# A hybrid decoder layer on one core: raw weights requested by GpSimd, twelve slots in the last passes, differences spread anew, another order in the first tile

## The chip, the cores and the metric

The kernel runs on one core of a Trainium2 chip. TensorE multiplies, ScalarE and VectorE prepare operands and work up results, GpSimd (POOL in the profile) helps them, SyncE (SP) requests most transfers. The metric is the device time of one execution in microseconds; lower is better.

## The reference

One inference step of a decoder layer for a prompt of 2048 tokens with 16 meta tokens, and for 8 samples of 8 tokens. The weights are the same for all; everything is fp32.

```python
h = rmsnorm(x, g_pre)
p = h @ w_in + b_in          # q_a k_a v_a z_a | q_m k_m v_m o_m z_m i_m f_m | g_a g_b
y_a = window_attention(q_a, k_a, v_a) * silu(z_a)     # 128 window, 16 meta keys, sinks
y_m = sigmoid(o_m) * mlstm(q_m, k_m, v_m, i_m, f_m) * silu(z_m)    # 4 heads of 256
merged = sigmoid(g_a) * (y_a @ w_pa) + sigmoid(g_b) * (y_m @ w_pb)
x = x + rmsnorm(merged @ w_out, g_post)
```

Returned are the new x of both groups, the window and meta keys and values, and the mLSTM states.

## The kernel before

**Stage 1** (to about 853 us) walks over the 17 tiles of 128 tokens: norm, projection of the attention's columns, attention. For the first tile ScalarE takes the mean square (`square`, L863) and the root (L865), VectorE scales a diagonal matrix with 1/root (`diagonal`, L1067), TensorE transposes the tile with it (`scale_row`, L1354), VectorE multiplies by g_pre (L1074), ScalarE rounds the result to fp32r (`split_made`, L873: the upper half), GpSimd takes input minus upper (`pool_split_h`, L298: the lower half), and TensorE multiplies upper by upper, upper by lower and lower by upper (L308 to L310; `block_b` 264 columns, `block_a` 384). The weights of the tile come in chunks, which ScalarE (L228) and VectorE split in the same way.

**Stage 2** (`stream`) is ten passes, each over all tokens with one weight matrix of 1024 by 1024: ZM, H0 to H3, GA, PA, GB, PB, OUT. Each computes a product by seven multiplications of quarter matrices in place of eight, 60 products a pass. A product is twelve matmuls of 128x512 on L2782, L2784 and L2785, in four quarters. During H0 to H3 the mLSTM of one head runs beside the products (for instance ScalarE's copy of the scores, L2365).

A pass needs seven weight blocks in the order T3, B22, B11, B21, T2, T1, T4, each in four units; unit x of a pass is x = 0 to 27. The B blocks are quarters of the weights, the T blocks are differences or sums of quarters. From H1 on the T blocks come from differences made in the kernel, in 64 chunks: ScalarE requests the four quarters of a chunk (`load_dif`), GpSimd subtracts four times (L2202 to L2208), ScalarE stores (`store_dif`). The list `DIF_AT` says beside which product.

A unit goes through these steps, each put at a product by a rule:

1. SyncE asks for the raw 256 KB into one of `NW` = 6 slots `waiting` (`load_unit`, L2023), after the slot's last user is lowered: `if v - NW >= RING: wait_unit(sp, v - NW)`.
2. ScalarE rounds it into the weight slot (L2297), once TensorE has left that slot: two units a product, from 6 products before the boundary (`unit_split_at`).
3. GpSimd (L2195) or VectorE (L2460) subtracts. In GB and OUT GpSimd has every second unit, in the other passes from H0 on every fourth (x = 3, 7, 11, ...); the rule is `lower_by_dve`.
4. TensorE waits for it before the quarter that uses it: T2 at product 5 of the pass, T1 (x = 20 to 23) at product 6, T4 at product 10.

Each engine's instructions stand in one fixed order, written by loops over the product number q. What waits in it holds up all behind it. SyncE's order has in addition the operands of the products (`next_operand`), three products ahead.

## Time and profile before

| | |
|---|---|
| median of 3 runs | 2869.46 us (2867.12 to 2875.72) |
| time of the profiled execution | 2862.34 us |
| its span, first to last instruction | 2860.3 us |
| mean granted TensorE clock | 0.987 |
| first product of ZM, H0, H1, H2, H3 | 857.2, 1016.2, 1257.0, 1495.7, 1733.7 us |
| first product of GA, PA, GB, PB, OUT | 1970.9, 2142.8, 2314.2, 2482.7, 2668.4 us |

The time of an execution is the span and what lies around it. Times of the trace are counted from the first instruction.

### The profile page before, as it was taken

What the parts mean: (1) busy time and instruction counts of PE and PEld (TensorE: products, weight loads), DVE (VectorE), ACT (ScalarE), POOL (GpSimd) and SP (SyncE); (2) the same over time, 40 slices, a digit from 0 to 9 for tenths busy, and PEclk for the clock granted to TensorE, in tenths of its full rate; (3) what the DMA queues carried; (4) which work ended last, traced back from release to release, by engine and by line L of the source; (5) the groups of instructions that cost most, each with busy time, mean ns of one, the idle gap of its engine ahead of it and who ended that gap; (6) DMA issues with size and microseconds to landing.
All of it is one profiled execution on the core that took longest, in us unless ns stands there. A gap on an engine that the chain in (4) does not pass through costs nothing.

```text
span 2860.3 us, 46433 instructions
## 1 busy us (share of the span) xinstructions
PE 2739.6 (96%) x15620; PEld 2285.6 (80%) x15620; DVE 1652.5 (58%) x4103; ACT 937.9 (33%) x2291; POOL 766.4 (27%) x1064
## 2 busy tenths in 40 slices
PE   6999999999999989999999999999999999999898
PEld 5888888888888767877886887888877878778686
DVE  5776665555653254465465556556247653577787
ACT  5774444444440021131122213114123231333443
POOL 3333533534540021132222223122000020122422
PEclk9999999999999999999999999999999999999999
DMA  8665565545777888898898889789786577956634
GB/s 302 237 223 165 174 207 190 184 166 191 235 225 260 284 303 264 268 333 256 279 291 299 263 286 319 252 263 321 252 293 212 184 276 242 325 194 220 221 142 152
DMA packets 410525, 697.46 MB, mean 244 GB/s; under 512 B 31778, under 2 KB 177575, under 8 KB 410260
## 3 DMA queue, kind: packets, MB, share of 16 engines
q1 hardware_dynamic: 298724, 526.72, 56.0%
q10 hardware_dynamic: 108848, 158.46, 16.2%
q0 software_dynamic: 2720, 9.32, 1.0%
q8 instruction: 128, 2.10, 0.3%
q14 instruction: 105, 0.86, 0.1%
HBM read 526.87 MB, written 169.48 MB: 243 GB/s over the span
## 4 chain that ended last, share of the span: by engine, by line
PE 56%; DMA 8%; DVE 2%; SPq 2%; issue 1%; ACT 1%; POOL 1%; ACTq 0%; POOLq 0%; DVEq 0%
PE bank_second L2782 7%; PE bank_second L2785 7%; PE bank_second L2784 7%; PE bank_third L2782 5%; PE bank_first L2782 5%; PE bank_third L2785 5%; PE bank_first L2785 5%; PE bank_third L2784 5%; PE bank_first L2784 5%; DMA st_waiting<-l_blocks_in 3%; DMA st_waiting<-difs_t 2%; PE st_bank_n L2830 2%; PE st_bank_u L2834 2%; DMA a_all<-sh_t 1%; DMA a_all<-hh_t 1%
## 5 line engine op out<-in xcount | busy, mean ns | idle before, releaser
L2782 PE MATMUL bank_second<-w_all,a_all 128*128 128x512 f32 x736 | 299.1, 406 | 7.0 <-DMA a_all<-sh_t 4.5
L2785 PE MATMUL bank_second<-w_all,a_all 128*128 128x512 f32 x736 | 289.2, 393 | 0.0
L2784 PE MATMUL bank_second<-w_all,a_all 128*128 128x512 f32 x736 | 288.6, 392 | 0.0
L2195 POOL TENSOR_TENSOR w_all<-st_waiting,w_all 128x512 fp32r<-128x512 f32 x57 | 79.3, 1393 | 607.6 <-ACT w_all L2297 607.6
L2365 ACT ACTIVATE mx_qkt<-st_bank_t 128x512 f32<-128x512 f32 x68 | 40.7, 599 | 570.8 <-PE st_bank_t L2805 565.4
L2782 PE MATMUL bank_third<-w_all,a_all 128*128 128x512 f32 x464 | 191.1, 412 | 25.1 <-POOL w_all L2195 10.5
L2782 PE MATMUL bank_first<-w_all,a_all 128*128 128x512 f32 x496 | 199.0, 401 | 8.7 <-DMA a_all<-hh_t 4.3
L2297 ACT ACTIVATE w_all<-st_waiting 128x512 fp32r<-128x512 f32 x184 | 110.4, 626 | 257.7 <-PE bank_first L2785 143.5
L2785 PE MATMUL bank_first<-w_all,a_all 128*128 128x512 f32 x496 | 193.7, 391 | 0.0
L2784 PE MATMUL bank_first<-w_all,a_all 128*128 128x512 f32 x496 | 193.2, 390 | 0.0
L2202 POOL TENSOR_TENSOR h_raw<-h_raw 128x256 f32<-128x256 f32 x64 | 50.2, 785 | 533.5 <-DMA h_raw<-l_blocks_in 533.5
L308 PE MATMUL bank_first<-w_all,a_all 128*128 128x384 f32 x544 | 189.3, 348 | 0.0
L2785 PE MATMUL bank_third<-w_all,a_all 128*128 128x512 f32 x464 | 183.6, 396 | 0.0
L2784 PE MATMUL bank_third<-w_all,a_all 128*128 128x512 f32 x464 | 183.1, 395 | 0.0
L309 PE MATMUL bank_first<-w_all,a_all 128*128 128x384 f32 x544 | 182.0, 335 | 0.0
L310 PE MATMUL bank_first<-w_all,a_all 128*128 128x384 f32 x544 | 182.0, 335 | 0.0
L924 ACT ACTIVATE at_sm<-at_sm,at_nmx 128x208 f32<-128x208 f32 x272 | 124.1, 457 | 153.8 <-DVE at_nmx L1145 153.7
L2782 PEld LDWEIGHTS bank_second<-w_all,a_all 128*128 128x128 f32 x736 | 139.6, 190 | 41.2 <-issue 6.4
L2785 PEld LDWEIGHTS bank_second<-w_all,a_all 128*128 128x128 f32 x736 | 139.3, 189 | 30.2
L2784 PEld LDWEIGHTS bank_second<-w_all,a_all 128*128 128x128 f32 x736 | 139.6, 190 | 27.1
L2516 DVE TENSOR_TENSOR st_u<-bank_second,st_t 128x512 f32<-128x512 f32 x80 | 55.1, 689 | 161.4 <-PE bank_second L2785 161.4
L317 PE MATMUL bank_third<-w_all,a_all 128*128 128x256 f32 (+1 forms) x480 | 147.7, 308 | 0.2 <-POOL a_all L298 0.2
(386 smaller groups left out, 7262.9 us busy)
## 6 DMA issues: line engine op xcount, KB each, us to landing
a_all<-sh_t SPq DMA_DIRECT2D x224, 512.0 KB, 5.2
a_all<-hh_t SPq DMA_DIRECT2D x180, 512.0 KB, 5.5
a_all<-hh_t ACTq DMA_DIRECT2D x104, 512.0 KB, 4.9
st_waiting<-difs_t SPq DMA_DIRECT2D x148, 256.0 KB, 6.9
h_raw<-l_blocks_in ACTq DMA_DIRECT2D x64, 512.0 KB, 5.6
difs_t<-h_raw ACTq DMA_DIRECT2D x64, 512.0 KB, 6.3
st_waiting<-l_blocks_in SPq DMA_DIRECT2D x108, 256.0 KB, 6.5
hh_t<-a_all SPq DMA_DIRECT2D x34, 512.0 KB, 6.1
```

What stands on the lines that cost most here:

```text
L308: nc.tensor.matmul(out, hi[:, j], k.w_hi[:, j, col:col + n], start=(j == 0), stop=False)
L309: nc.tensor.matmul(out, hi[:, j], k.w_lo[:, j, col:col + n], start=False, stop=False)
L310: last = nc.tensor.matmul(out, lo[:, j], k.w_hi[:, j, col:col + n], start=False, stop=(j == KT - 1))
L317: nc.tensor.matmul(out, hi[:, j], k.w_hi[:, j, col:col + n], start=(j == 0), stop=False)
L924: nc.scalar.activation(sm[:, g, :], sm[:, g, :], ACT.Exp, bias=nmx[:, g:g + 1], scale=HD ** -0.5, accum_out=rs[:, g:g + 1]).then_inc(exp_r ...
L2195: G.tensor_tensor(unit_half(v, 1), unit_view(v), unit_half(v, 0).bitcast(F32), ALU.subtract).then_inc(k.lower_done, 1)
L2297: A.activation(unit_half(v, 0), unit_view(v), ACT.Copy).then_inc(k.upper_done, 1)
L2782: T.matmul(bank_view(bank, at), hi, weight_row(k, at, 0, t), start=fresh and t == 0, stop=False, skip_group_check=True)
L2784: T.matmul(bank_view(bank, at), hi, weight_row(k, at, 1, t), start=False, stop=False, skip_group_check=True)
L2785: last = T.matmul(bank_view(bank, at), lo, weight_row(k, at, 0, t), start=False, stop=t == KH - 1, skip_group_check=True)
L2830: T.matmul(p_n[:, 0:MD + 1], qat[:, j, :], cn[:, h % 2, j, :], start=(j == 0), stop=False)
L2834: q = T.matmul(p_u[j][:, 0:MD + 1], kw[:, j * P:(j + 1) * P], vaug(n), start=True, stop=True)
```

## The change

It has four parts.

- **Requests.** `load_unit` moves from SyncE to GpSimd, where it stands ahead of the lower halves of the same product.
- **Tail.** From PA on there are twelve raw slots (six more in memory which the mLSTM has left), the rounding takes three units a product, the lower half stands one product after the rounding, and the requests of the first twelve units start at product 40 of the pass before.
- **Differences.** 14 chunks stand in H0 at products 6, 9, ..., then 16, 15, 15 in H1 to H3 from product 8 on, one in 2.8 products, and 4 in GA. Load and store stand 2 products to either side of the subtractions, not 3.
- **First tile.** ScalarE takes one root of a constant first. Its splitting of chunk 4 comes before `square(1)`, and VectorE's of chunks 2 and 3 before `diagonal(1)`. TensorE runs a block as eight matmuls upper by upper, eight upper by lower, eight lower by upper, the last in step with GpSimd's pairs.

The diff, cut to these parts:

```diff
@@ -751,7 +752,10 @@
             pool.wait_ge(ones_set, 1)
-            pool_split_h(nc, k, 0, 0, None)
+            pool.wait_ge(k.h_hi_ready, 1)
+            for j in range(0, KT, 2):
+                q = nc.gpsimd.tensor_tensor(k.h_lo[:, 0, j:j + 2], k.h_raw[:, 0, j:j + 2], k.h_hi[:, 0, j:j + 2].bitcast(F32), ALU.subtract)
+                q.then_inc(first_lo if j + 2 < KT else k.h_lo_ready, 1)
             pool_split_h(nc, k, 1, 1, None)
@@ -877,16 +881,16 @@
             act.wait_ge(eps_set, 1)
+            nc.scalar.activation(sd[:, 1:2], eps[:, 0:1], ACT.Sqrt)
             square(0)
...
             split_made(0, None)
-            for c in range(2, 4):
+            for c in range(2, 5):
                 act_split_chunk(nc, k, c)
             square(1)
-            act_split_chunk(nc, k, 4)
             split_made(1, None)
@@ -1082,10 +1086,10 @@
                             ALU.subtract).then_inc(gate_lo, 1)
-            dve_split_chunk(nc, k, 1)
+            for c in range(1, 4):
+                dve_split_chunk(nc, k, c)
             diagonal(1)
-            for c in range(2, 5):
-                dve_split_chunk(nc, k, c)
+            dve_split_chunk(nc, k, 4)
             normed(1)
@@ -1398,10 +1402,29 @@
             pe.wait_ge(ones_set, 1)
+            def first_block(out, col, n, chunks, between):
+                hi, lo = k.h_hi[:, 0], k.h_lo[:, 0]
+                pe.wait_ge(k.w_hi_ready, chunks)
+                pe.wait_ge(k.h_hi_ready, 1)
+                for j in range(KT):
+                    T.matmul(out, hi[:, j], k.w_hi[:, j, col:col + n], start=(j == 0), stop=False)
+                between()
+                pe.wait_ge(k.w_lo_ready, chunks)
+                for j in range(KT):
+                    T.matmul(out, hi[:, j], k.w_lo[:, j, col:col + n], start=False, stop=False)
+                for j in range(KT):
+                    if j % 2 == 0 and j + 2 < KT:
+                        pe.wait_ge(first_lo, j // 2 + 1)
+                    elif j % 2 == 0:
+                        pe.wait_ge(k.h_lo_ready, 1)
+                    last = T.matmul(out, lo[:, j], k.w_hi[:, j, col:col + n], start=False, stop=(j == KT - 1))
+                return last
             scale_row(0)
-            block_b(0, 0, 0, True)
-            scale_row(1)
-            block_a(0, 0, 0, True)
+            pe.wait_ge(gate_hi, 1)
+            first_block(p_b[:, 0:W + GATES], attn_base(0) + ZC, W + GATES, k.AT[0] + 2, lambda: pe.wait_ge(gate_lo, 1)).then_inc(proj_b, 1)
+            first_block(p_a[:, 0:ZC], attn_base(0), ZC, k.AT[0] + 5, lambda: scale_row(1)).then_inc(proj_a, 1)
             scale_row(2)
@@ -1595,7 +1618,13 @@
 LOADED_AHEAD = 3
-DIF_AT = {c: N_PROD * H0 + 4 + ((c - DIF_FIRST) * 9 // 2 if c < DIF_FIRST + 8 else 37 + (c - DIF_FIRST - 8) * 18 // 5) for c in range(DIF_FIRST, N_DIF)}
+TAIL = N_UNIT * PA
+DIF_LEAD = 2
+DIF_PLACES = [N_PROD * H0 + 6 + 3 * i for i in range(14)]
+for _s, _n in ((H1, 16), (H2, 15), (H3, 15)):
+    DIF_PLACES += [N_PROD * _s + 8 + i * 14 // 5 for i in range(_n)]
+DIF_PLACES += [N_PROD * GA + 14 + 8 * i for i in range(4)]
+DIF_AT = {c: DIF_PLACES[c - DIF_FIRST] for c in range(DIF_FIRST, N_DIF)}
 DIF_NOW = {q: c for c, q in DIF_AT.items()}
@@ -1752,7 +1781,31 @@
         return -3 if x < EARLY + KH else 5 + (x - EARLY - KH) // 2
-    return N_PROD * s - 6 + x // 2
+    return N_PROD * s - 6 + (x // 3 if s >= PA else x // 2)
+def unit_lowered_at(v):
+    return unit_split_at(v) + (1 if v >= TAIL else 0)
+def waiting_slot(v):
+    return (v - TAIL) % (2 * NW) if v >= TAIL else (v - RING) % NW
+def former_unit(v):
+    before = v - 2 * NW if v - 2 * NW >= TAIL else v - NW
+    if v >= TAIL and v - 2 * NW < TAIL:
+        before = v - NW if v < TAIL + NW else None
+    return before if before is not None and before >= RING else None
+def unit_landed(v):
+    turns = 0
+    while v is not None:
+        turns, v = turns + 1, former_unit(v)
+    return 16 * turns
@@ -1766,12 +1819,16 @@
         return -4 if x < RING + NW else unit_split_at(v) - 1
+    if s >= PA:
+        return N_PROD * (s - 1) + 40 + x if x < 2 * NW else unit_split_at(v) - 2
     return N_PROD * (s - 1) + 46 + x if x < NW else unit_split_at(v) - 1
-SPLITS_AT, LOADS_AT = {}, {}
+SPLITS_AT, LOWERS_AT, LOADS_AT = {}, {}, {}
 for _v in range(EARLY, N_UNITS):
     SPLITS_AT.setdefault(unit_split_at(_v), []).append(_v)
+    LOWERS_AT.setdefault(unit_lowered_at(_v), []).append(_v)
     if _v >= RING:
@@ -2012,15 +2071,6 @@
                     load_operand(sp, k, q)
-            def load_unit(v):
-                s, block, kt = v // N_UNIT, NEEDED[v % N_UNIT // KH], v % KH
-                if 2 * KH * s >= DIF_FIRST and block not in RAW_OF:
-                    for out in dif_out:
-                        sp.wait_ge(out, 16 * (KH * s + kt - DIF_FIRST // 2 + 1))
-                if v - NW >= RING:
-                    wait_unit(sp, v - NW)
-                sp.dma_start(waiting[:, (v - RING) % NW], unit_source(k, v)).then_inc(unit_in[(v - RING) % NW], 16)
@@ -2195,6 +2243,21 @@
+            def load_unit(v):
+                s, block, kt = v // N_UNIT, NEEDED[v % N_UNIT // KH], v % KH
+                if 2 * KH * s >= DIF_FIRST and block not in RAW_OF:
+                    for out in dif_out:
+                        pool.wait_ge(out, 16 * (KH * s + kt - DIF_FIRST // 2 + 1))
+                if former_unit(v) is not None:
+                    wait_unit(pool, former_unit(v))
+                at = waiting_slot(v)
+                if v == TAIL + NW:
+                    pool.wait_ge(state_out, 16 * (MH + 2))
+                    pool.wait_ge(cs_out, 16 * NB * MH)
+                    for i in range(2):
+                        pool.wait_ge(y_out[i], 16 * N_TILES // 2)
+                pool.dma_start(waiting[:, at] if at < NW else more_waiting[:, at - NW], unit_source(k, v)).then_inc(unit_in[at], 16)
             def differences(c):
@@ -2242,10 +2307,12 @@
                         finish(g, row)
+                for v in LOADS_AT.get(q, ()):
+                    load_unit(v)
                 if q == N_PROD * PB:
...
                         load_pa(N_ITEM * PB + row, 0 if row == 0 else 1)
-                for v in SPLITS_AT.get(q, ()):
+                for v in LOWERS_AT.get(q, ()):
                     if not lower_by_dve(v):
@@ -2411,10 +2478,10 @@
                         A.activation(t1[:, :], bank_x[:, :], ACT.Copy).then_inc(t1_ready, 1)
-                if q + 3 in DIF_NOW:
-                    load_dif(DIF_NOW[q + 3])
-                if q - 3 in DIF_NOW:
-                    store_dif(DIF_NOW[q - 3])
+                if q + DIF_LEAD in DIF_NOW:
+                    load_dif(DIF_NOW[q + DIF_LEAD])
+                if q - DIF_LEAD in DIF_NOW:
+                    store_dif(DIF_NOW[q - DIF_LEAD])
                 mixer_first(q)
```

How this moves instructions, at three places.

GpSimd at the change from H0 to H1, before (`w_all` and `w_early` are the weight slots, `h_raw` the two buffers of the differences, L2195 a lower half):

```order
L2195 TENSOR_TENSOR w_all<-st_waiting,w_all 128x512
L2202 TENSOR_TENSOR h_raw<-h_raw 128x256
L2204 TENSOR_TENSOR h_raw<-h_raw 128x256
L2206 TENSOR_TENSOR h_raw<-h_raw 128x256
L2208 TENSOR_TENSOR h_raw<-h_raw 128x256
L2195 TENSOR_TENSOR w_all<-st_waiting,w_all 128x512
L2195 TENSOR_TENSOR w_early<-st_waiting,w_early 128x512
L2202 TENSOR_TENSOR h_raw<-h_raw 128x256
L2204 TENSOR_TENSOR h_raw<-h_raw 128x256
L2206 TENSOR_TENSOR h_raw<-h_raw 128x256
L2208 TENSOR_TENSOR h_raw<-h_raw 128x256
```

and now (L2243 is the lower half, L2259 a request; the first row is x = 3):

```order
L2243 TENSOR_TENSOR w_all<-st_waiting,w_all 128x512
L2259 DMA st_waiting<-l_blocks_in 128x512 x4
L2243 TENSOR_TENSOR w_all<-st_waiting,w_all 128x512
L2259 DMA st_waiting<-l_blocks_in 128x512 x4
L2243 TENSOR_TENSOR w_early<-st_waiting,w_early 128x512
L2259 DMA st_waiting<-l_blocks_in 128x512 x2
L2259 DMA st_waiting<-difs_t 128x512 x2
L2243 TENSOR_TENSOR w_all<-st_waiting,w_all 128x512
L2259 DMA st_waiting<-difs_t 128x512 x4
L2243 TENSOR_TENSOR w_early<-st_waiting,w_early 128x512
L2259 DMA st_waiting<-difs_t 128x512 x4
L2243 TENSOR_TENSOR w_all<-st_waiting,w_all 128x512
```

The subtractions have left the boundary, and between two lower halves stand the four requests of the next group.

GpSimd in OUT, before, around its first final addition (L2233):

```order
L2195 TENSOR_TENSOR w_early<-st_waiting,w_early 128x512 x2
L2195 TENSOR_TENSOR w_all<-st_waiting,w_all 128x512 x3
L2227 TENSOR_TENSOR st_c<-st_c,st_e 128x1024
L2195 TENSOR_TENSOR w_all<-st_waiting,w_all 128x512 x2
L2227 TENSOR_TENSOR st_c<-st_c,st_e 128x1024
L2195 TENSOR_TENSOR w_all<-st_waiting,w_all 128x512 x2
L2233 TENSOR_TENSOR st_e<-st_c,st_e 128x1024
L2195 TENSOR_TENSOR w_all<-st_waiting,w_all 128x512
L2195 TENSOR_TENSOR w_all<-st_waiting,w_all 128x2x256 x2
```

and now (L2243 a lower half, L2290 the addition that belongs to PB, L2296 the final addition):

```order
L2259 DMA st_more_waiting<-difs_t 128x512 x3
L2243 TENSOR_TENSOR w_all<-st_more_waiting,w_all 128x512
L2259 DMA st_more_waiting<-difs_t 128x512 x3
L2243 TENSOR_TENSOR w_all<-st_waiting,w_all 128x512 x2
L2259 DMA st_waiting<-difs_t 128x512 x3
L2243 TENSOR_TENSOR w_all<-st_waiting,w_all 128x512
L2290 TENSOR_TENSOR st_c<-st_c,st_e 128x1024
L2259 DMA st_waiting<-difs_t 128x512
L2243 TENSOR_TENSOR w_all<-st_more_waiting,w_all 128x512 x3
L2290 TENSOR_TENSOR st_c<-st_c,st_e 128x1024
L2243 TENSOR_TENSOR w_all<-st_waiting,w_all 128x2x256 x2
L2296 TENSOR_TENSOR st_e<-st_c,st_e 128x1024 x17
```

All lower halves of the pass stand ahead of the first final addition; before, three stood behind it.

ScalarE at the start, before:

```order
L863 ACT_TABLE_LOAD
L863 ACTIVATE w_plain,at_ss<-w_plain 128x4x256
L865 ACT_TABLE_LOAD
L865 ACTIVATE at_sd<-at_ss,at_eps 128x1
L882 ACTIVATE w_all<-scan_wif 128x8x8
L228 ACTIVATE w_all<-stage 128x8x128 x2
L873 ACTIVATE a_all<-h_raw 128x1024
L228 ACTIVATE w_all<-stage 128x8x128 x2
L863 ACTIVATE w_plain,at_ss<-w_plain 128x4x256
L865 ACTIVATE at_sd<-at_ss,at_eps 128x1
L228 ACTIVATE w_all<-w_plain 128x8x128
```

and now:

```order
L884 ACT_TABLE_LOAD
L884 ACTIVATE at_sd<-at_eps 128x1
L867 ACTIVATE w_plain,at_ss<-w_plain 128x4x256
L869 ACTIVATE at_sd<-at_ss,at_eps 128x1
L887 ACTIVATE w_all<-scan_wif 128x8x8
L228 ACTIVATE w_all<-stage 128x8x128 x2
L877 ACTIVATE a_all<-h_raw 128x1024
L228 ACTIVATE w_all<-stage 128x8x128 x2
L228 ACTIVATE w_all<-w_plain 128x8x128
L867 ACTIVATE w_plain,at_ss<-w_plain 128x4x256
```

The second table load is gone and the first stands ahead of the first input; chunk 4 (`w_all<-w_plain`) went ahead of the second tile's square. TensorE's first rows now are:

```order
L1358 MATMUL bank_second<-w_plain,at_ones 128x128
L1411 MATMUL bank_third<-w_all,a_all 128x264 x8
L1415 MATMUL bank_third<-w_all,a_all 128x264 x8
L1421 MATMUL bank_third<-w_all,a_all 128x264 x8
L1411 MATMUL bank_first<-w_all,a_all 128x384 x8
L1358 MATMUL at_bank_pp<-w_plain,at_ones 128x128
L1415 MATMUL bank_first<-w_all,a_all 128x384 x8
L1421 MATMUL bank_first<-w_all,a_all 128x384 x8
```

Before, L308, L309 and L310 took turns through all eight parts of both blocks.

## Rows read from the trace of the kernel before

**Rows 1.** The page: busy time by engine.

```profile
PE 2739.6 (96%) x15620; PEld 2285.6 (80%) x15620; DVE 1652.5 (58%) x4103; ACT 937.9 (33%) x2291; POOL 766.4 (27%) x1064
```

**Rows 2.** Windows of the weight passes, columns in the first row.

```profile
core 0: us, PE busy (x) PEld busy (x) DVE busy (x) ACT busy (x) POOL busy (x), PEclk, DMA share, GB/s
970.00:990.00 20.00, 17.92 (x73) 14.31 (x72) 4.31 (x7) 0.00 (x0) 0.00 (x0) 0.91 1.02 364
1013.00:1053.00 40.00, 32.70 (x138) 24.33 (x140) 20.48 (x32) 16.05 (x29) 13.00 (x14) 1.00 1.03 371
1130.00:1145.00 15.00, 11.36 (x43) 9.12 (x43) 4.83 (x13) 2.18 (x6) 2.93 (x4) 0.77 0.71 251
1255.00:1285.00 30.00, 26.03 (x116) 21.48 (x115) 18.32 (x37) 11.75 (x26) 15.87 (x16) 0.94 1.05 381
...
1970.00:2000.00 30.00, 30.00 (x144) 24.98 (x143) 22.39 (x42) 14.89 (x28) 10.33 (x9) 1.00 0.99 364
2143.00:2175.00 32.00, 27.68 (x114) 22.11 (x114) 26.66 (x39) 17.76 (x31) 6.94 (x5) 0.95 0.69 249
2325.00:2350.00 25.00, 21.66 (x92) 16.77 (x92) 11.75 (x14) 8.87 (x13) 6.40 (x5) 1.00 0.85 310
2490.00:2520.00 30.00, 25.16 (x104) 19.37 (x103) 23.31 (x33) 14.00 (x25) 8.72 (x6) 0.94 0.76 285
2670.00:2710.00 40.00, 28.16 (x115) 21.60 (x114) 29.28 (x32) 18.80 (x33) 20.05 (x12) 0.83 0.61 202
```

**Rows 3.** TensorE's waits, 1255 to 1285 and 2670 to 2710: total, times, longest.

```profile
PE st_bank_n L2814 <- ACT mx_qkt L2365: 4.0, 1, 4.0
...
PE bank_third L2782 <- POOL w_all L2195: 10.5, 2, 6.3
```

**Rows 4.** The chain of waits, 1255 to 1285: start, length, what.

```profile
1265.68 8.17 DMA difs_t<-h_raw
```

**Rows 5.** Timeline of GpSimd around OUT: start, length, work, idle before.

```profile
2650.93 1.33 POOL L2195 TENSOR_TENSOR w_early<-st_waiting,w_early 128x512 fp32r<-128x512 f32 x1 [1.96 <-ACT w_early L2297]
...
2698.56 2.38 POOL L2233 TENSOR_TENSOR st_e<-st_c,st_e 128x1024 f32<-128x1024 f32 x1 [5.75 <-DVE st_c L2577]
```

**Rows 6.** Requests by GpSimd itself: duration in ns, and us to landing.

```profile
L2216 POOL DMA_DIRECT2D st_e<-pa_t x17: 540/567/604, 2485.4 to 2658.2; - x17
...
DMA to landing us min/median/max: 3.7/4.6/7.8
```

**Rows 7.** The page, costliest groups: lower half and rounding of a unit.

```profile
L2195 POOL TENSOR_TENSOR w_all<-st_waiting,w_all 128x512 fp32r<-128x512 f32 x57 | 79.3, 1393 | 607.6 <-ACT w_all L2297 607.6
...
L2297 ACT ACTIVATE w_all<-st_waiting 128x512 fp32r<-128x512 f32 x184 | 110.4, 626 | 257.7 <-PE bank_first L2785 143.5
```

**Rows 8.** The page, transfers: raw units, KB each, us to landing.

```profile
st_waiting<-difs_t SPq DMA_DIRECT2D x148, 256.0 KB, 6.9
```

**Rows 9.** Timelines of GpSimd and TensorE, start of H1 and of GA.

```profile
1246.77 1.29 POOL L2195 TENSOR_TENSOR w_all<-st_waiting,w_all 128x512 fp32r<-128x512 f32 x1 [4.62 <-ACT w_all L2297]
...
1286.91 0.39 PE L2782 MATMUL bank_third<-w_all,a_all 128*128 128x512 f32 x1
...
1971.37 1.31 POOL L2195 TENSOR_TENSOR w_early<-st_waiting,w_early 128x512 fp32r<-128x512 f32 x1 [8.60 <-ACT w_early L2297]
...
1994.96 0.39 PE L2782 MATMUL bank_third<-w_all,a_all 128*128 128x512 f32 x1
```

**Rows 10.** Timelines of ScalarE, GpSimd, TensorE and VectorE, first tile.

```profile
7.94 1.28 ACT L865 ACT_TABLE_LOAD   x1
...
11.73 1.06 ACT L228 ACTIVATE w_all<-stage 128x1024 fp32r<-128x1024 f32 x1 [0.73 <-DMA stage<-l_chunks_in]
...
14.58 3.77 POOL L298 TENSOR_TENSOR a_all<-h_raw,a_all 128x256 fp32r<-128x256 f32 x4 [8.67 <-ACT a_all L873]
...
18.60 0.56 PE L308 MATMUL bank_third<-w_all,a_all 128*128 128x264 f32 x1 [7.56 <-POOL a_all L298]
...
29.31 0.16 DVE L1057 TENSOR_TENSOR scan_gates<-bank_third,scan_bif 128x8 f32<-128x8 f32 x1
```

More of the change, by code:

```diff
@@ L1832, in stream @@
         raw_in = [sem("raw_in0"), sem("raw_in1")]
-        unit_in = [sem(f"unit_in{i}") for i in range(NW)]
+        unit_in = [sem(f"unit_in{i}") for i in range(2 * NW)]
         lower_done_dve = sem("lower_done_dve")
@@ L1992, in unit_view @@
                 return staged_unit(k, v)
[L1993 removed]
+            at = waiting_slot(v)
+            return (waiting[:, at] if at < NW else more_waiting[:, at - NW]).rearrange("p (i n) -> p i n", n=LW // 2 if slot_of(v) == 6 else P)
         def unit_half(v, part):
@@ L2130, in _ @@
             for q in range(-4, Q_ALL + 8):
-                for v in LOADS_AT.get(q, ()):
-                    load_unit(v)
                 if 6 <= q + LOADED_AHEAD < Q_ALL:
@@ L2235, in _ @@
             G.memset(eps, EPS).then_inc(eps_set, 1)
-            for v in SPLITS_AT[-3]:
+            for v in LOADS_AT[-4]:
+                load_unit(v)
+            for v in LOWERS_AT[-3]:
                 if not lower_by_dve(v):
@@ L2718, in _ @@
                         norm_row(g, row)
-                for v in SPLITS_AT.get(q if q != 4 else -3, ()) if q >= 0 else ():
+                for v in LOWERS_AT.get(q if q != 4 else -3, ()) if q >= 0 else ():
                     if lower_by_dve(v):
```

7 lines of the change are left out of this document (5 added, 2 removed).

## The prediction

> **What bounds the kernel now.** I read the totals first. TensorE is busy 96% of the span [rows 1], at a mean granted clock of 0.987 (the table above), so at most some 120 us are to be had: idle time, and time in which the clock stood at the lower of its two levels. Next I looked for TensorE's idle time by place. Half of it lies in the first attention stage, which the change touches only at its first tile. In the second stage it lies in a few short stretches, nearly all where one weight pass follows another. I asked for these stretches in one table [rows 2]. The loss of a stretch is its length less TensorE's busy time, plus (1 - granted clock) times its length, since a mean clock of 0.83 leaves 17% of the full-speed work undone. Example: 2670 to 2710 gives 40.00 - 28.16 + 0.17 x 40 = 18.6 us. Likewise: end of ZM 3.9; start of H0 7.3; inside H0 7.1; H1 5.8 (H2 and H3, whose rows repeat H1's, 6.0 and 5.6); GA 0; PA 5.9; GB 3.3; PB 6.6; OUT 18.6.
>
> Then the waits. At OUT TensorE waits 10.5 us for GpSimd's lower halves, and at H1 4.0 us for ScalarE [rows 3]. The chain of waits says why ScalarE was late: it stood 8.17 us behind the store of a difference [rows 4]. It is to wait for a difference's transfer inside its one order of work, and the raw weights of the same stretch come through it too. GA's boundary, the one after a head with no differences beside it, loses nothing [rows 2]. At OUT GpSimd stood 5.75 us in front of the first final addition, and lower halves that TensorE needed stood behind it in GpSimd's order [rows 5].
>
> **The change, part by part.** A boundary works like this: a raw unit is requested, lands, ScalarE rounds it, VectorE or GpSimd makes the lower half, the slot is free. With SyncE as requester this ran as a pipe six slots deep. With GpSimd as requester the order shows groups: four requests stand between two of its lower halves, so no request of the next group starts before GpSimd has lowered the last unit of the group before. In passes up to GA the boundary is thus a chain of cycles: about 0.3 us wait, 0.57 for the first request [rows 6], the next landing (call it L), 0.63 rounding, 0.1, and 1.39 lowering [rows 7], together 3.0 + L.
>
> L is what the trace does not show: a 256 KB piece by GpSimd's queue beside a full load of 370 to 380 GB/s [rows 2]. Nearest below is GpSimd's own request of 512 KB pieces in calmer stretches, 3.7 us at best, 4.6 in the middle, 7.8 at worst [rows 6]. Nearest above is the same piece through SyncE, 6.9 us in the middle, which includes standing behind operands in SyncE's queue [rows 8]. I take 5.0, near the lower, since a queue of its own has nothing ahead of the piece; both ends stay for the range. A cycle is then 8 us.
>
> *GA*: the twelfth unit was lowered by 1972.7, three cycles bring the 24th at 1996.7, and TensorE needs it at 1994.96 [rows 9]. Loss 1.8 and some clock: 0 becomes 3. *H1*: the eighth unit ends at 1248.1, four cycles give 1280.1. TensorE needed it at 1286.91 [rows 9]; without the 4.0 wait and half of the clock's loss (1.8) it would be there at 1281.1. So the units come in time with 1 us to spare. The ScalarE stop goes too, as no difference now lies in a head's products 0 to 7 (the first is at 8, so its load is asked for at 6). H2 and H3 are built alike. I leave 1.1 us at each: 17.4 becomes 3.4, **gain 14**. *H0*: no slack, because the first differences lie at its sixth product and GpSimd's chain ends 1.4 us later than what stands there: 7.3 becomes 9, **loss 1.7**; GA **loss 3**.
>
> *Tail (PA to OUT)*. Twelve slots hold three blocks of raw weights before the boundary. They are requested from product 40 on, when slots have long been free, and the rounding is spread over three units a step. At PA the losses were waits for halves by VectorE which came late behind late landings; I leave 1 us of 5.9, **gain 4.9**. GB: its halves come in time in the same way, but a burst of twelve transfers beside the operands can make one operand late: 3.3 becomes 1.3, **gain 2**. PB 6.6 becomes 1.0, **gain 5.6**. *OUT*: GpSimd's work up to its 23rd unit is twelve lower halves (16.7 us), two additions (5.6), sixteen requests at 0.57 + 0.3 (13.9) and one more load, about 37 us; from 2651, where the first unit is lowered [rows 5], that ends at 2688, about when TensorE asks. And the order shows every lower half of OUT ahead of the first final addition. I leave 5 of 18.6, **gain 13.6**. If this cover failed, 6.3 us [rows 3], the longest single wait, would come back.
>
> *SyncE relieved*. At the end of ZM TensorE waits for an operand which SyncE asks for late, being stopped in front of a weight slot. This goes: **gain 3** of 3.9. Inside H0 the late operand has no weight request ahead of it, so the 7.1 there stays, and denser differences (one in 2.8 products in place of 3.6) add transfers in the heads: **loss 2.1**, an estimate of half a late operand. The requests themselves (256 units of 0.57 = 146 us on GpSimd, busy 27% [rows 1]) lie in GpSimd's idle time, except at the boundaries, where they are counted.
>
> *First tile*. TensorE starts at 18.60 after 7.56 us of waiting for GpSimd, whose four subtractions took 3.77 us from 14.58; before that two table loads of 1.28 us stood in ScalarE's chain [rows 10]. Now one load is taken before the input arrives and the other is gone, which is worth 2.5 until the second chunk of weights, there at 11.7, limits it. So VectorE and ScalarE start the rounding of the inputs 0.5 earlier (12.8), TensorE starts at 14.0 on the rounded halves, GpSimd's halves follow by twos, and both blocks end 4.5 us earlier. VectorE took them off at 29.31 [rows 10], behind the preparation of the next tiles, whose inputs are no earlier; I take 26.2. **Gain 3** (1 to 4.5).
>
> *Sum*: 3 + 3 - 1.7 - 2.1 + 14 - 3 + 4.9 + 2 + 5.6 + 13.6 = 39.3 us. The profiled execution took 2862.34, so its like would take 2823. The median of the runs is 2869.46, 7.1 above that one execution, so I give **2830 us**.
>
> A rule speaks against this L. In "DMA: Bandwidth & Descriptors", section "Issuing engines are not separate DMA queues", the Trainium skill says that transfers of all issuing engines run on the same 16 DMA engines, and that issuing from several saves only sequencer time. By that rule L would be SyncE's 6.9, and rival B below would be the outcome. The 4.6 us for twice the bytes speaks against it, but comes from a stretch with less traffic, so the trace does not decide.
>
> **The rivals.** *A, the requests are slower than 5 us.* L of 6 to 6.5 puts 4 to 6 us on each chain of four. H1 to H3 have 1 us to spare, H0 and GA none, so 17 to 27 us come back and the gain is 12 to 22: 2847 to 2857, say 2850. For: the 7.8 us [rows 6], and stretches at 380 GB/s [rows 2]. Against: the median there.
>
> *B, GpSimd's requests land no sooner than SyncE's.* L = 6.9 makes a cycle of 9.9 and a chain of 39.6, 7.6 longer than the forecast's. Against before, H0 comes out 9.3 worse and with the clock that falls in so long a stop some 13, H1 to H3 3 each (7.6 less the spare 1, and some clock, in place of the 5.8 that goes), GA 9: together -31, against +30 in the start, ZM and the tail: 2870, no change. For: SyncE's row is the only one of the same piece in the same stretches [rows 8]. Against: 4.6 us for twice the bytes [rows 6].
>
> *C, the other side.* The same chain, priced: five boundaries, four cycles, so 1 us on L costs 20 us less the spare, about 19. Slower by 0.3% (8.6 us) is decided from L = 7.4 on. At 7.8, the worst seen [rows 6], the cost is 17 us: 2887. For: a boundary's traffic is denser than where GpSimd's own requests stand, and one of the seventeen took 7.8. Against: sixteen others.
>
> The Trainium skill, "SBUF — State Buffer", its box on the "DVE blocks DMA" trap, says that a transfer requested on GpSimd's queue starves while VectorE runs a copy in its two-port mode (some 620 ns alone, 3100 beside a copy). The median of 4.6 us [rows 6], taken beside VectorE's additions, shows nothing of it, and VectorE's work at a boundary is mostly two-operand; by that rule C would hold only where copies stand.
>
> *D, the change does not do what it says.* If ScalarE's stop at the heads has another cause (its order is dense there), the 14 shrink to 4: 2840, inside A's span.
>
> **How the numbers follow.** Forecast 0.60, A with D 0.20, B 0.11, C 0.09. Faster by over 0.3% holds the forecast and A: 0.80; within 0.3%, which is what this kernel's runs (2867.12 to 2875.72) can tell from no change, 0.11; slower 0.09. The range: the start's bounds (1 to 4.5), OUT's (6 more or 5 less), L from 3.7 (H0 and GA free, another 9 us) and the 7 us between execution and median reach down to 2807; upward it takes in A and reaches to 2861, short of B. The likeliest case alone spans 2812 to 2842.
>
> **What would show it.** First product of the first tile at 14 us, first evictions at 26. In H1 to H3, no wait for ScalarE's copy of scores in the first eight products; loads by GpSimd landing 5 us after issue; GpSimd's 24th unit of GA near 1996 relative to before. At OUT no wait over 2 us for lower halves. I am wrong if loads of a group take 7 us, if TensorE waits at +5 and +6 of each head for halves, or if GpSimd, stopped in front of a slot, holds back a subtraction that ScalarE waits for.

## The result, and the profile after

The changed kernel takes 2884.33 us (median of 14 runs, 2874.04 to 2888.69), the kernel before 2868.32 us in the same comparison (14 runs, 2863.70 to 2875.72). The ratio is 1.005, 95% interval 1.0039 to 1.0062: 16 us slower, where I had forecast 38 us faster. The profiled execution has a span of 2884.7 us.

The page of the changed kernel: busy time by engine, and its weight requests.

```profile
PE 2754.8 (95%) x15620; PEld 2297.3 (80%) x15620; DVE 1665.6 (58%) x4103; ACT 937.1 (32%) x2291; POOL 891.4 (31%) x1320
...
st_waiting<-difs_t POOLq DMA_DIRECT2D x118, 256.0 KB, 6.0
...
st_waiting<-l_blocks_in POOLq DMA_DIRECT2D x84, 256.0 KB, 6.8
```

TensorE is busy 95%, as against 96% [rows 1]. A request of GpSimd's lands after 6.0 or 6.8 us (5.5 and 7.6 for the six further slots; median of all 256 is 6.4), where I had put 5.0 and SyncE had 6.9 [rows 8].

The length of each pass (from its first product to the next pass's first product in the trace, us; s1 is stage 1), worked out from the same rows of the two traces and of seven of the experiments:

| | s1 | ZM | H0 | H1 | H2 | H3 | GA | PA | GB | PB | OUT |
|---|---|---|---|---|---|---|---|---|---|---|---|
| before | 857.2 | 159.0 | 240.8 | 238.7 | 238.1 | 237.2 | 171.9 | 171.3 | 168.5 | 185.7 | 191.9 |
| after | 859.8 | 162.8 | 245.6 | 236.7 | 237.2 | 234.9 | 189.1 | 163.3 | 185.1 | 178.6 | 191.5 |
| E3, differences | 860.4 | 161.3 | 241.0 | 231.4 | 231.6 | 230.7 | 171.5 | 170.9 | 170.0 | 186.5 | 192.1 |
| E1, SyncE requests | 856.1 | 157.5 | 241.6 | 232.4 | 232.6 | 230.7 | 175.6 | 167.0 | 174.7 | 186.3 | 185.1 |
| E4, GpSimd requests alone | 860.1 | 163.2 | 251.5 | 242.7 | 242.1 | 247.6 | 191.3 | 176.5 | 179.9 | 187.4 | 199.4 |
| E5, GpSimd to GA | 856.6 | 158.4 | 246.2 | 237.6 | 236.9 | 234.6 | 175.5 | 170.0 | 171.0 | 186.7 | 184.9 |
| E6, GpSimd from PA on | 856.4 | 160.0 | 241.3 | 232.8 | 232.9 | 230.7 | 181.5 | 163.3 | 178.9 | 182.2 | 191.7 |
| E7, two a step | 858.8 | 161.8 | 238.1 | 235.2 | 233.0 | 230.7 | 169.8 | 167.7 | 167.4 | 180.2 | 192.4 |
| E12, unchained | 855.2 | 160.7 | 240.9 | 233.1 | 232.6 | 230.7 | 177.1 | 170.2 | 165.3 | 193.2 | 185.0 |

The loss is in two passes: GA is 17.2 us longer and GB 16.6. Most of it lies where the sum had charged nothing, at the ends of both, and at GB's start, where it had put a gain. PA and PB are 8.0 and 7.1 shorter, a little more than forecast. H1 to H3 give 5.2 in place of 14, OUT 0.4 in place of 13.6.

Windows of the changed kernel, in the columns of [rows 2]:

```profile
core 0: us, PE busy (x) PEld busy (x) DVE busy (x) ACT busy (x) POOL busy (x), PEclk, DMA share, GB/s
1268.00:1310.00 42.00, 39.51 (x194) 29.82 (x193) 24.06 (x49) 16.15 (x33) 18.82 (x26) 1.00 0.89 300
1977.00:2012.00 35.00, 32.18 (x141) 25.70 (x140) 20.52 (x41) 13.28 (x25) 13.34 (x19) 0.95 0.84 285
2130.00:2166.00 36.00, 28.01 (x114) 22.42 (x113) 20.62 (x27) 14.17 (x23) 13.89 (x20) 0.91 0.83 294
2329.00:2370.00 41.00, 33.41 (x132) 26.74 (x131) 24.46 (x21) 9.54 (x14) 22.21 (x28) 0.88 0.91 328
2490.00:2514.00 24.00, 15.84 (x61) 12.32 (x61) 16.59 (x20) 10.19 (x18) 14.38 (x22) 0.86 0.96 342
2693.00:2735.00 42.00, 30.84 (x127) 24.39 (x126) 35.33 (x37) 19.71 (x35) 23.54 (x20) 0.88 0.47 166
```

Reckoned as in the forecast: start of H1 2.5, start of GA 4.6, end of GA 7.99 + 3.2 = 11.2, start of GB 12.5, end of GB 11.5, OUT 16.2 us. Before, the starts of H1, GA and GB lost 5.8, 0 and 3.3, and OUT 18.6 [rows 2]. TensorE's longest waits from ZM on (total, times, longest):

```profile
PE bank_second L2849 <- DMA a_all<-hh_t: 13.0, 3, 5.5
PE bank_third L2849 <- DMA a_all<-sh_t: 10.3, 4, 2.7
PE st_bank_t L2800 <- POOL st_c L2290: 6.8, 2, 5.7
...
PE bank_first L2849 <- DVE st_c L2554: 5.0, 1, 5.0
```

Before, the first place was the 10.5 us for lower halves [rows 3]. These are gone. In their place stand operands (a_all) that land late, an addition of GpSimd's at OUT, and one wait for VectorE of 5.0 us.

The start came as forecast. GpSimd's subtractions, TensorE's first products, VectorE's first eviction in the changed kernel:

```profile
14.25 4.84 POOL L757 TENSOR_TENSOR a_all<-h_raw,a_all 128x256 fp32r<-128x256 f32 x4 [8.36 <-ACT a_all L877]
...
14.21 2.10 PE L1411 MATMUL bank_third<-w_all,a_all 128*128 128x264 f32 x8 [5.82 <-ACT a_all L877]
...
26.79 0.16 DVE L1061 TENSOR_TENSOR scan_gates<-bank_third,scan_bif 128x8 f32<-128x8 f32 x1
```

TensorE begins at 14.21 (forecast 14.0) and VectorE evicts at 26.79 (26.2), against 18.60 and 29.31 [rows 10]; the later tiles' mean squares start 1.9 us earlier than before.

### The profile page after: what moved, and what is told of

Same layout as the page of the kernel before. It is cut to its first block and busy times, and to the rows that moved or that the text cites. A ratio compares the mean times of both kernels' runs of the same rounds, so it can differ in the third digit from the quotient of the medians.

```text
span 2884.7 us, 46426 instructions
## 1 busy us (share of the span) xinstructions
PE 2754.8 (95%) x15620; PEld 2297.3 (80%) x15620; DVE 1665.6 (58%) x4103; ACT 937.1 (32%) x2291; POOL 891.4 (31%) x1320
## 3 DMA queue, kind: packets, MB, share of 16 engines
q10 hardware_dynamic: 108848, 158.46, 16.2%
## 5 line engine op out<-in xcount | busy, mean ns | idle before, releaser
L2243 POOL TENSOR_TENSOR w_all<-st_waiting,w_all 128x512 fp32r<-128x512 f32 x39 | 52.0, 1335 | 457.4 <-ACT w_all L2364 453.5
L308 PE MATMUL bank_first<-w_all,a_all 128*128 128x384 f32 x536 | 186.5, 348 | 0.0
L309 PE MATMUL bank_first<-w_all,a_all 128*128 128x384 f32 x536 | 179.4, 335 | 0.0
L310 PE MATMUL bank_first<-w_all,a_all 128*128 128x384 f32 x536 | 179.4, 335 | 0.0
L2364 ACT ACTIVATE w_all<-st_waiting 128x512 fp32r<-128x512 f32 x138 | 83.1, 626 | 245.7 <-PE bank_first L2852 141.6
```

What stands on the lines that cost most here:

```text
L308: nc.tensor.matmul(out, hi[:, j], k.w_hi[:, j, col:col + n], start=(j == 0), stop=False)
L309: nc.tensor.matmul(out, hi[:, j], k.w_lo[:, j, col:col + n], start=False, stop=False)
L310: last = nc.tensor.matmul(out, lo[:, j], k.w_hi[:, j, col:col + n], start=False, stop=(j == KT - 1))
L2243: G.tensor_tensor(unit_half(v, 1), unit_view(v), unit_half(v, 0).bitcast(F32), ALU.subtract).then_inc(k.lower_done, 1)
L2364: A.activation(unit_half(v, 0), unit_view(v), ACT.Copy).then_inc(k.upper_done, 1)
```

## The experiments

Each time is a median on the same chip as the kernel before, which lay between 2867.0 and 2869.1 us in these comparisons. E1 to E4, E5 to E8, E9 to E11, and E12 with E13 were timed together, each group on another chip. Between these groups the kernel before moves by up to 2 us, so a difference across groups is uncertain by about as much. "E1" is the changed kernel with all requests given back to SyncE.

**E1, SyncE requests.**

```diff
             for q in range(-4, Q_ALL + 8):
+                for v in LOADS_AT.get(q, ()):
+                    load_unit(v)        # with sp. in place of pool., and gone from GpSimd
                 if 6 <= q + LOADED_AHEAD < Q_ALL:
```

> The changed kernel with its weight requests given back to SyncE, at the same products; twelve slots, differences and first tile stay as changed. Theory Q (queues share): a request on GpSimd's queue does not stand behind the operands of SyncE's queue but beside them and takes its share of the 16 engines from them, so the operands of the last products of GA and GB land late (waits of 8 us in each, 16 us landing). Then these waits go here and the time is 2850 to 2860, below the kernel before. Theory S (schedule): three units a product ask for more than the transfers can carry, whoever requests; then the waits at the ends of GA and GB stay within 2 us and the time is 2878 to 2886.

Measured 2841.37 us, ratio 0.990 (0.9882 to 0.9918). The move of the requests alone costs 2884.3 - 2841.4 = 43 us, more than the whole loss. GA's end has 2.1 us of waiting where the changed kernel has 8.0, but at GB's end 6.7 us stay. The time lies below both ranges, so neither theory holds alone.

**E2, the first tile alone** (the diff's first four pieces on the kernel before).

> The kernel before with the first tile's new order alone. The trace after shows the following tiles 1.9 us earlier, so 2866 to 2867 (gain 2) if what was lost later in stage 1 (4.6 us in dips of the granted clock) is chance; 2870 or more if the new order brings these dips with it.

Measured 2866.94 us, ratio 0.999 (0.9978 to 1.0003). The 2 us agree with the trace, but the comparison can't tell them from nothing.

**E3, the differences alone.**

```diff
-DIF_AT = {c: N_PROD * H0 + 4 + ...}
+DIF_AT = {c: DIF_PLACES[c - DIF_FIRST] for c in range(DIF_FIRST, N_DIF)}
...
-                if q + 3 in DIF_NOW:
+                if q + DIF_LEAD in DIF_NOW:
```

> The kernel before with the new places of the differences alone, SyncE requesting, six slots. If the stop of ScalarE at the starts of H1 to H3 was the cost that I priced at 14 us, and the chain of GpSimd's requests took the rest of it away in the changed kernel, this gives 12 to 14: 2855. If the boundaries of the heads have another limit, the gain is the 5 us that the changed kernel shows in H1 to H3, or less: 2863 to 2868.

Measured 2844.89 us, ratio 0.9913 (0.9893 to 0.9933): 24 us, 10 more than the upper expectation. H1 to H3 are 20.3 us shorter in the profiled execution. E3's first 34 us around H1's start:

```profile
1256.00:1290.00 34.00, 34.00 (x162) 28.35 (x161) 23.93 (x50) 15.38 (x30) 5.35 (x4) 1.00 0.99 344
```

TensorE is busy without a gap at full clock, with 344 GB/s of transfers beside it. Before, the same place lost 4.0 us to ScalarE and had a clock of 0.94 [rows 2, 3]. ScalarE's own wait in front of that work, 1255 to 1285 in the kernel before, was

```profile
ACT mx_qkt L2365 <- DMA difs_t<-h_raw: 5.4, 1, 5.4
```

and at H2's start it stood 4.8 us for a store as well. In E3 it waits for no store at H1's start. E3 also takes the transfers of the differences out of these stretches (344 GB/s in place of 381), and no run tells the two effects apart.

**E4, GpSimd's requests alone**, with six slots and the old differences.

```diff
-                sp.dma_start(waiting[:, (v - RING) % NW], unit_source(k, v))...
+                pool.dma_start(waiting[:, (v - RING) % NW], unit_source(k, v))...
```

> The kernel before with the weight requests moved to GpSimd alone, six slots, old places of the differences. Theory Q: operands late at the ends of ZM, GA and GB, and the chain of request and lowering at each boundary, 10 to 25 us slower (2880 to 2893). Theory S: the move costs nothing at the ends of the passes, at most 5 us at the boundaries (2868 to 2873).

Measured 2941.46 us, ratio 1.0248 (1.0224 to 1.0272): 72.5 us slower, about three times the most that either theory gave. TensorE's waits from ZM on:

```profile
PE bank_third L2784 <- POOL w_all L2184: 19.1, 7, 7.0
PE st_bank_n L2832 <- DVE mx_wqk L2588: 13.4, 5, 5.1
PE st_bank_n L2816 <- ACT mx_qkt L2367: 13.0, 4, 4.4
PE bank_third L2784 <- DMA a_all<-sh_t: 11.8, 4, 4.4
```

Lower halves of GpSimd's lead, and then the mixer's work on VectorE and ScalarE. GpSimd has the requests, a quarter of the halves (half of them in GB and OUT) and the subtractions of the differences in one order, and each waits for the one ahead. In the changed kernel the last of the three is out of the way at the boundaries. That this explains why it loses 43 us and not 72 is argued, not shown. E4 has late operands too: it waits 5.8 us at GA's last two products and 3.2 at GB's, against 1.7 and 0 before.

**E5, GpSimd requests up to GA only**, SyncE from PA on (`if v < TAIL:` and `if v >= TAIL:` ahead of the two calls).

> The changed kernel with GpSimd requesting the weights of the passes up to GA only and SyncE those of PA to OUT (its own semaphores for the two). The time between E1 (all by SyncE, 2841) and the changed kernel (2884) is to be shared out. If the chain of request and lowering at the boundaries costs what the passes show (ZM to H3 are 17 to 22 us shorter in E1), this gives 2858 to 2866. If only the ends of GA and GB count, it gives 2841 to 2846.

Measured 2864.36 us, ratio 0.9993 (0.9981 to 1.0005), 23 us above E1. H0 to H3 are 18.0 us longer than E1's.

**E6, the counterpart: GpSimd requests from PA on.**

> The counterpart: SyncE requests up to GA, GpSimd from PA on. Theory Q: operands late by 8 us at the end of GA, GpSimd's late halves and additions around PB and OUT, together 15 to 25 us more than E1: 2857 to 2866. Theory S, by which the queue is no matter: 2841 to 2845.

Measured 2850.52 us (2841.59 to 2860.69), ratio 0.9943 (0.9923 to 0.9964), 9 us above E1 and between the two expectations. Parts of 23 and 9 make 32 (25 and 11, if each time is taken against the kernel before of its own group); the other 8 to 11 of the 43 appear only when both stand together. The table places them, though it doesn't explain them: against E1, GA and GB are 13.5 and 10.4 us longer in the changed kernel, where the changes of E5 and E6 add up to 5.8 and 0.5, and PA and PB take 7 of that back.

**E7, two units a step in the tail.** E1, with

```diff
-    return N_PROD * s - 6 + (x // 3 if s >= PA else x // 2)
+    return N_PROD * s - 6 + x // 2
...
-    return unit_split_at(v) + (1 if v >= TAIL else 0)
+    return unit_split_at(v)
```

> E1 with its tail's rounding at two units a product and the lower half beside it, as in the kernel before; twelve slots and early requests stay. In E1 the waits for the last operand of GA and GB (2.1 and 6.7 us) and for VectorE at PA's and PB's product 58 (3.4 and 5.0 us) were new against the kernel before. If three units a product made them, they go and the waits at products 5 and 6 come back only in part: 2830 to 2838. If the early requests made them: 2840 or more.

Measured 2834.17 us, ratio 0.9886 (0.9871 to 0.9901), 7 us below E1. The end of GB in E1, and in E7:

```profile
2440.00:2468.00 28.00, 21.17 (x85) 16.77 (x84) 17.28 (x24) 13.21 (x22) 6.67 (x6) 0.88 0.96 345
```

```profile
2440.00:2462.00 22.00, 20.18 (x88) 16.01 (x87) 15.44 (x21) 9.69 (x17) 4.56 (x4) 1.00 0.93 338
```

The waits for the last operands fall from 6.7 to 1.8 us and the clock stays up, at about the same GB/s. In SyncE's order the pieces of a product stand ahead of its operand, three in E1 and two in E7. GA and GB together are 13.1 us shorter than E1's. OUT goes back to 192.4, with its 10.5 us for lower halves behind the final addition, so three a step was worth something there alone.

**E8, every fourth half in GB and OUT too.** E1, with

```diff
-    return kt != 3 if s - 1 in STREAMED else kt % 2 == 1
+    return kt != 3
```

> E1 with GpSimd making every fourth lower half in GB and OUT too, not every second. Theory L (lock): a VectorE instruction that meets GpSimd's subtractions one behind another does not end before them (6.02 us for a lower half of 0.68 at PB's end, 7.15 for a scaling of 1.3 in the changed kernel); with half of them the longest VectorE instruction stays under 3 us and PB's wait of 5.0 us goes: 2834 to 2840. If VectorE's work is what delays, seven more halves of 0.68 us each at these two boundaries make it 2842 to 2850.

Measured 2836.61 us, ratio 0.9896 (0.9882 to 0.9910), 5 us below E1 (3 against the kernels before). No VectorE instruction is held longer than 2.3 us beyond its own time (5.3 in E1), and PB's wait falls from 5.0 to 3.0; in turn TensorE's wait for VectorE at OUT's fifth product grows from 1.8 to 4.5.

**E9, E7 with OUT's last eight halves by VectorE.**

```diff
+    if s == OUT and v % N_UNIT >= 20:
+        return True
     return kt != 3 if s - 1 in STREAMED else kt % 2 == 1
```

> E7 with OUT's last eight lower halves (T1 and T4) all made by VectorE, so that none stands on GpSimd behind the first final addition. In E7 TensorE still waits 4.3 and 6.3 us there. If GpSimd's place in its order is the cause, both waits go and some clock comes back: 2820 to 2825. If the halves are late because the pieces land late, VectorE makes them no sooner: 2832 or more.

Measured 2826.49 us, ratio 0.9857 (0.9837 to 0.9876), 8 us below E7 and 1.5 above the range of the first case. The waits of 4.3 and 6.3 us for GpSimd are gone, 3.6 us for VectorE's halves stand in their place, and OUT is 188.1.

**E10, E7 with GpSimd requesting from PA on.**

> E7 with the requests from PA on moved to GpSimd, the rate staying at two units a product. Theory Q: TensorE waits for operands at products 58 and 59 of GA and GB again (none and 1.8 us in E7, 8 us in the changed kernel), with operand landings of over 12 us; GA and GB 5 to 10 us longer each, 2845 to 2860. Theory S: only three units a product make operands late; GA stays at 170 and GB at 167 to 169, 2834 to 2839.

Measured 2856.81 us, ratio 0.9963 (0.9951 to 0.9976), 23 us above E7, but not where theory Q had put it. The waits at GA's products 58 and 59 are 1.7 us, not 8. In the profiled executions GA is 5.7 longer, PA 8.2 and PB 7.5, at lower halves of VectorE's that come late (waits up to 2.4 us) and an addition of GpSimd's (2.1); what delays each of them no run shows.

**E11, E9 with H0's differences from product 12 on** (`N_PROD * H0 + 12 + 3 * i`).

> E9 with H0's differences from product 12 on, not 6. H0 still loses 11 us, half of it at products 0 to 9. If the transfers of the differences crowd out operands and weights there, as they did in H1 to H3, H0 becomes 4 to 7 us shorter: 2815 to 2819. If the operands of product 1 and the first weights are late for their own bytes, nothing changes: 2820 to 2825.

Measured 2822.67 us, ratio 0.9839 (0.9823 to 0.9856), 4 us below E9 and the fastest here. H0 is 236.4 against 238.7: 2.3 us, less than the 4 to 7 of the first theory, and the time lies in the range of the second. So the differences cost H0 little or nothing. The ranges of E9 and E11 overlap (2822.34 to 2829.93, and 2820.55 to 2824.36).

**E12, E5 without the chain**: GpSimd requests up to GA, VectorE makes all halves of H0 to GA.

```diff
-    return kt != 3 if s - 1 in STREAMED else kt % 2 == 1
+    return H0 <= s <= GA or (kt != 3 if s - 1 in STREAMED else kt % 2 == 1)
```

> E5 (GpSimd requests up to GA, 2864) with all lower halves of H0 to GA made by VectorE, so that no lower half of GpSimd's stands between its groups of requests and nothing but a free slot holds them up. Chain theory (my forecast's cycle of request, landing, rounding and lowering is what GpSimd's requests cost in the heads): H1 to H3 go back from 237.6, 236.9, 234.6 to about 232 each, H0 by 4, less what seven more halves of 0.68 cost VectorE: 2842 to 2850. Queue theory (the own queue, not the chain): 2860 to 2868.

Measured 2844.12 us, ratio 0.9917 (0.9902 to 0.9932), 20 us below E5.

**E13, the control: the same halves, SyncE requesting.**

> The control: the same moved halves with SyncE requesting everything, that is E1 with all lower halves of H0 to GA on VectorE. What differs between it and E12 is the queue and the requester alone. E1 is 2841; if VectorE carries the halves freely, 2838 to 2845; if they delay its mixer work, 2846 to 2855, and that much is to be taken off E12.

Measured 2838.01 us, ratio 0.9894 (0.9876 to 0.9913), 3.4 us below E1. So 20.2 - 3.4 = 17 us of E5's 23 are the chain (some 19 of 25, each against its own kernel before), and 2844.1 - 2838.0 = 6 us the requester and its queue. In the profiled executions E12's passes H0 to H3 add up to 937.3 us, exactly E1's; GA is 4.9 longer than in E13. The median landing of GpSimd's requests is the same with the chain and without (6.2 and 6.4 us): it was not the landing that cost, but that something stood behind it.

## Why the prediction was wrong

**What bounds the kernel.** Right: the starts of the passes. E3 bears out that the place of the differences was the cost, and its trace fits the chain that I read [rows 4]: the store of a difference held ScalarE, and ScalarE held TensorE. The term was too small. I forecast 14 us at H1 to H3; alone, the differences give 24, since in each head some 7 us go, the mixer's waits and the clock with them.

**L and the cycle.** "I take 5.0": 6.0 and 6.8 were measured. GpSimd at the start of GA in the changed kernel, lower halves (L2243) and requests (L2259):

```profile
1976.58 1.28 POOL L2243 TENSOR_TENSOR w_early<-st_waiting,w_early 128x512 fp32r<-128x512 f32 x1 [5.05 <-ACT w_early L2364]
1977.80 1.10 POOL L2259 DMA_DIRECT2D st_waiting<-l_blocks_in  x2
1978.90 1.06 POOL L2259 DMA_DIRECT2D st_waiting<-difs_t  x2
1985.18 1.29 POOL L2243 TENSOR_TENSOR w_all<-st_waiting,w_all 128x512 fp32r<-128x512 f32 x1 [5.22 <-ACT w_all L2364]
1986.42 2.16 POOL L2259 DMA_DIRECT2D st_waiting<-difs_t  x4
1993.85 1.27 POOL L2243 TENSOR_TENSOR w_early<-st_waiting,w_early 128x512 fp32r<-128x512 f32 x1 [5.28 <-ACT w_early L2364]
1995.07 2.20 POOL L2259 DMA_DIRECT2D st_waiting<-difs_t  x4
2003.26 1.28 POOL L2243 TENSOR_TENSOR w_all<-st_waiting,w_all 128x512 fp32r<-128x512 f32 x1 [5.99 <-ACT w_all L2364]
```

The cycles have the forecast's make and take 8.6, 8.7 and 9.4 us in place of 8. GpSimd stands 5 to 6 us in front of each half, as it can ask for nothing while it waits. Its 24th unit is ready 27.5 us after GA's start where 25.8 was forecast, and the start loses 4.6 in place of 3. This is rival A's price: L of 6 to 6.5 was to bring back 17 to 27 us, and as requester up to GA GpSimd costs 23 (E5 against E1), of which the chain is 17. Rival B's condition was met as well: over all 256 requests the median landing is 6.4 us by GpSimd in the changed kernel and 6.5 by SyncE in E1. A queue of its own did not make the pieces land sooner on the whole. Yet neither rival reaches 2884; the rest lies from GA's end on.

**The steps that failed: GpSimd's price as requester, and the tail.** In the sum the requests were +3 at ZM, -1.7 at H0 and -3 at GA, a net loss of 1.7 us; they cost 43 (E1). That is the larger error. It has three parts: the chain up to GA, which I had seen and priced too low; what the requests do at the ends of the passes, where the sum had no term; and GpSimd's order in the tail, where the sum counted the requests' 13.9 us at OUT only as a time that fits.

For the tail the sum said "Twelve slots hold three blocks of raw weights before the boundary" and took only gains: 4.9, 2, 5.6 and 13.6, 26 in all. With SyncE requesting, what is left for the tail when first tile and differences are taken off is a gain of 1.5 us; in the changed kernel the passes from GA on are 18.3 us longer than before. The starts of PA and PB gained what was said. But only the term for GB asked which transfers the extra pieces would stand beside, and left it inside 1.3 us. They stand at the end of the pass before. In GA and GB SyncE must bring one operand of 512 KB for each product. Three units of 256 KB a product on top of it are 1.31 MB in 2.72 us (twelve matmuls, 0.227 us apart in the rows), 482 GB/s, where [rows 2] never show over 381; two units make 386. I had these rows and did not divide. The division marks where to look and no more: E1 has the three units too and waits only 2.1 us at GA's end.

The late operand of GA's last product in the changed kernel, requested by SyncE at 2144.87, beside GpSimd's piece of the same time (KB each, us to landing):

```profile
a_all<-hh_t SPq DMA_DIRECT2D x1, 512.0 KB, 16.4
st_waiting<-l_blocks_in POOLq DMA_DIRECT2D x1, 256.0 KB, 6.9
```

The same operand in E4 (GpSimd too, but two units a product as before), in E1, and in E10:

```profile
a_all<-hh_t SPq DMA_DIRECT2D x1, 512.0 KB, 16.6
```

```profile
a_all<-hh_t SPq DMA_DIRECT2D x1, 512.0 KB, 9.6
```

```profile
a_all<-hh_t SPq DMA_DIRECT2D x1, 512.0 KB, 10.0
```

The landing of the last operand of GA and of GB in all the traces, by schedule of the tail and by who requests there (us):

| | GA, SyncE | GA, GpSimd | GB, SyncE | GB, GpSimd |
|---|---|---|---|---|
| six slots, two a product | 9.8, 10.2, 9.8 | 16.6 | 7.5, 10.1, 9.0 | 12.7 |
| twelve slots, three | 8.0 to 9.7 (five) | 16.4, 13.8 | 9.0 to 14.3 (five) | 16.5, 10.6 |
| twelve slots, two | 5.5, 5.7, 5.8 | 10.0 | 10.2, 6.7, 7.5 | 5.4 |

At GA the operand lands 4 to 8 us later where GpSimd requests, in each of the three schedules, and with twelve slots the third unit a product adds 2 to 6 with either requester. Late operands at GA's end therefore do not need three units a product: E4 has them with two. At GB kernels with the same instructions there differ by 3 to 6 us, so a single landing there decides nothing. A piece asked for at the same time overtakes the operand, 6.9 us against 16.4. The Trainium skill, "DMA: Bandwidth & Descriptors", section "Queues, rings and completion order", says that each of the transfer engines takes turns between the queues that have work. The trace fits this: GpSimd's piece does not stand behind the operands in SyncE's queue. I had written "a queue of its own has nothing ahead of the piece". That is so, and the operands paid for it. The page's other rule, cited in the prediction, that issuing engines are not separate transfer capacity, agrees with the medians of 6.4 and 6.5 us.

**OUT.** Forecast 13.6, came 0.4. The halves did get ahead of the final addition, and with SyncE's requests OUT and PB together gain 6.2 us (E1). With GpSimd's requests TensorE waits 5.7 us at OUT's second product for an addition of GpSimd's; it is 5.9 in E4 and E6, and under 1 us in all the others. And the halves now stand one behind another on GpSimd, which has a price that the sum did not have, shown clearest at GB's start. VectorE's rows in the changed kernel, and GpSimd's of the same time:

```profile
2335.88 7.15 DVE L2533 SCALAR_TENSOR_TENSOR st_c<-st_e,st_c 128x1024 f32<-128x1024 f32 x1
2342.95 1.75 DVE L2527 TENSOR_TENSOR w_all<-st_more_waiting,w_all 128x512 fp32r<-128x512 f32 x1
2344.62 0.68 DVE L2554 TENSOR_TENSOR st_c<-bank_first,st_bias 128x512 f32<-128x512 f32 x1
```

```profile
2336.37 1.31 POOL L2243 TENSOR_TENSOR w_all<-st_more_waiting,w_all 128x512 fp32r<-128x512 f32 x1
2337.62 0.55 POOL L2259 DMA_DIRECT2D st_more_waiting<-difs_t  x1
2338.19 1.30 POOL L2243 TENSOR_TENSOR w_all<-st_more_waiting,w_all 128x512 fp32r<-128x512 f32 x1
2339.45 2.49 POOL L2243 TENSOR_TENSOR w_early<-st_waiting,w_early 128x512 fp32r<-128x512 f32 x2
2342.26 1.90 POOL L2243 TENSOR_TENSOR w_all<-st_waiting,w_all 128x512 fp32r<-128x512 f32 x1 [0.32 <-ACT w_all L2364]
```

A scaling of 1.3 us takes 7.15: it is issued just ahead of the first of four subtractions (the third row is two) and ends at 2343.03, 1.1 us after the fourth. The fifth then takes 1.90 in place of 1.3: now it is the one that is held. TensorE waits 5.0 us for the eviction behind the scaling. E6 repeats both figures (7.15 and 5.1). In E1 a lower half of 0.68 us is caught in the same way:

```profile
2637.02 6.02 DVE L2525 TENSOR_TENSOR w_early<-st_waiting,w_early 128x512 fp32r<-128x512 f32 x1
```

With half as many halves on GpSimd (E8) nothing is held for more than 2.3 us, beside a single addition. At OUT's start the same thing happens twice in the changed kernel (4.5 and 5.0 us for instructions of 0.7 and 1.3).

What these cases share is more than the run of subtractions. VectorE's instruction began while GpSimd was in a transfer request: at 2335.88 in the one of 2335.82 to 2336.36, and in E1 at 2637.02 in the one of 2636.84 to 2637.42. The same holds for 16 of the 17 VectorE instructions from ZM on which were held for over 2.6 us in all the traces. I counted the other side as well: of some 580 VectorE instructions with both operands in SBUF that began during a subtraction or addition of GpSimd's with at least two more right behind it, all but one got in after the first. So a run of subtractions alone does not shut VectorE out; a request with a run behind it can. No run varied this by itself.

**SyncE relieved: gain 3 at ZM.** Wrong: ZM is 3.8 longer in the changed kernel, and the late operand at its product 48 is in every run (1.7 to 3.7 us), whoever requests weights. No weight request was ahead of it. At ZM's last product there is even a new wait for an operand, 1.8 to 2.8 us in the four kernels in which GpSimd requests there (the changed one, E4, E5, E12) and at most 0.4 in the others. The pass as a whole lies between 157.5 and 163.5 us in kernels that do not differ there, so the 3.8 as such says little.

**First tile: gain 3.** 1.9 in the trace. Stage 1 nevertheless ends between 855 and 862 us in all kernels alike, with dips of the granted clock that come and go, so I read nothing into the 2.6 by which it was longer after.

**The account**, in medians: first tile -2, differences -24, tail with SyncE's requests 2841.4 - 2842.9 = -1.5, GpSimd as requester +43; sum +15.5, measured +16. The tail's -1.5 is what is left over, as no run has the tail alone, so that the sum comes out is no proof of it. In the forecast the same four were -3, -11.9, -26.1 and +1.7. Open: the 8 to 11 us that E5 and E6 do not add up to, and the split of the 23 us of E10. That the two queues share by turns is my reading of the landings; no run measured it by itself.

## What to carry to other kernels

Before requests are moved to another engine, write down what stands behind them in its order: an engine that requests, and then works on what it requested, runs at the pace of one landing per group, however early the buffers are free; and look at which urgent transfers of the other queue the requests will now run beside. When loads are spread differently, charge the bytes per step to the stretch where they now fall, and compare with the highest rate that the trace shows; the gain at the start of a stage is only worth what its predecessor can spare. Test a change of four parts in its parts: here one was worth 24 us, and another cost 43.
